# S5 parameter set-up beside the projections, modulation rows in four column tiles, and three smaller edits in a hybrid diffusion step

## The reference

```python
mod = silu(cond) @ ada_w[l] + ada_b[l]                  # two conditions: c_ctx and c
proj = h @ ev_w_in                                      # layer 0: 2048 columns
# S5: 32 groups of 16 channels, 64 complex states, two directions
lam_bar = exp(lam * exp(log_step)); b_bar = ((lam_bar - 1) / lam) * B
bu = b_bar @ u;  hs = scan(lam_bar, bu);  y = Re(C @ hs) + d * u
y = gelu(y);  y = y * sigmoid(y @ glu_w + glu_b)
# mLSTM, per head, direction and chunk of 128 tokens
dmat = where(causal, b[t] - b[s] + i[s], -inf)
s = (q @ k.T) * exp(dmat - mq);  num = s @ v + w_inter * (q @ cm)
cm_new = keep * cm + (w_s * k).T @ v                    # the final states are outputs too
```

## Time and profile before

| | us |
|---|---|
| median of 3 runs | 5072.52 (5072.29 to 5074.31) |
| the profiled execution | 5074.22 |
| its span | 5072.4 |
| PE busy | 4520.9 (89%) |
| DVE busy | 2916.7 (58%) |
| POOL busy | 1705.2 (34%) |
| ACT busy | 799.7 (16%) |

### The profile page before, as it was taken

One profiled execution on the slowest core, in us unless ns is written; L12 is line 12 of the kernel. 1 busy time (PEld: TensorE's weight loads), 2 busy tenths in 40 slices (PEclk: granted clock), 3 DMA queues, 4 the chain that ended last, 5 costly groups with the idle time before them and its releaser, 6 DMA issues. The chain is left out here.

```text
span 5072.4 us, 43983 instructions
## 1 busy us (share of the span) xinstructions
PE 4520.9 (89%) x15098; PEld 2543.0 (50%) x15098; DVE 2916.7 (58%) x5806; ACT 799.7 (16%) x1626; POOL 1705.2 (34%) x1616
## 2 busy tenths in 40 slices
PE   6798766897799999999997998688879999999997
PEld 2453233475645545555444677456655555555453
DVE  4424752298636756665684405449853765666477
ACT  1211232103700000000002213110550000000000
POOL 0000541003805645555550000000551565555464
PEclk8899988899999999999998998799999999999998
DMA  3120423112638989999891110221454998999896
GB/s 135 46 81 31 146 86 123 66 55 89 178 133 322 368 312 394 353 365 351 335 370 59 66 42 0 54 75 46 133 170 160 351 367 331 378 366 351 305 404 270
DMA packets 354240, 1048.43 MB, mean 207 GB/s; under 512 B 31689, under 2 KB 132505, under 8 KB 342330
## 3 DMA queue, kind: packets, MB, share of 16 engines
q0 software_dynamic: 148128, 545.35, 28.4%
q1 hardware_dynamic: 106844, 450.27, 24.0%
q10 hardware_dynamic: 99072, 50.33, 3.5%
HBM read 991.70 MB, written 54.14 MB: 206 GB/s over the span
## 5 line engine op out<-in xcount | busy, mean ns | idle before, releaser
L598 PE MATMUL banks<-blocks,dense_weight 128*128 128x512 f32 x3072 | 1377.4, 599 | 51.3 <-DVE dense_weight L773 51.3
L565 PE MATMUL banks<-h_dense_T,blocks 128*128 128x384 f32 x4096 | 1363.6, 487 | 37.7 <-DVEq L666 37.7
L565 PEld LDWEIGHTS banks<-h_dense_T,blocks 128*128 128x128 f32 x4096 | 779.8, 191 | 628.8 <-issue 111.3
L598 PEld LDWEIGHTS banks<-blocks,dense_weight 128*128 128x128 f32 x3072 | 589.3, 192 | 755.3 <-issue 697.0
L409 POOL DMA_INDIRECT expert_rows<-in_pk_u_dram,expert x512 | 649.4, 1268 | 797.4 <-DVE own_dots L788 352.1
L409 POOL DMA_INDIRECT expert_rows<-in_pk_v_dram,expert x512 | 601.1, 1174 | 491.2 <-DVE acc L807 203.0
L773 DVE TENSOR_TENSOR dense_weight<-dense_act,shared 128x384 f32<-128x384 f32 x256 | 218.4, 854 | 802.4 <-PE banks L598 738.1
L807 DVE SCALAR_TENSOR_TENSOR acc<-expert_rows,expert_weight,acc 128x1024 f32<-128x1024 f32 x504 | 624.4, 1284 | 64.6 <-DMA expert_rows<-in_pk_v_dram,expert 64.1
L788 DVE CUSTOM_DVE_ANT_0 expert_rows<-expert_rows,h_rows 128x1024 f32<-128x1024 f32 x512 | 595.0, 1221 | 0.1
L444 ACT ACTIVATE dense_act<-banks 128x384 f32<-128x384 f32 x256 | 125.5, 490 | 2356.5 <-PE banks L565 2346.7
L400 POOL TENSOR_SCALAR shared<-iota,picked_T 128x128 f32<-128x128 f32 x192 | 120.6, 642 | 522.2 <-ACT picked_T L450 460.3
(11 more groups left out here) (461 smaller groups left out, 4660.9 us busy)
## 6 DMA issues: line engine op xcount, KB each, us to landing
blocks<-in_pk_u_turned_dram SPq DMA_DIRECT2D x256, 512.0 KB, 6.3
blocks<-in_pk_v_dram SPq DMA_DIRECT2D x256, 512.0 KB, 6.8
gates_dram<-shared ACTq DMA_DIRECT2D x48, 1024.0 KB, 5.1
shared<-gates_dram SPq DMA_DIRECT2D x32, 1536.0 KB, 10.8
ada_block<-in_ada_rest_dram SPq DMA_DIRECT2D x32, 1280.0 KB
blocks<-in_pk_w_q_dram SPq DMA_DIRECT2D x32, 512.0 KB, 3.6
w_block<-in_ev_w_in_dram SPq DMA_DIRECT2D x16, 512.0 KB, 3.5
expert_rows<-in_pk_u_dram,expert POOLq DMA_INDIRECT x512, 7.8
```

Source lines behind the costliest of these rows:

```text
L565: mm = pe.matmul(dense_dots(c), u[:, k * P:(k + 1) * P], HT[:, k, :], start=(k == 0), stop=(k == KD - 1))
L598: mm = pe.matmul(ps[:, at_:at_ + HALF], wt[:, c % WEIGHED, z * P:(z + 1) * P], v[:, half_ * HALF:(half_ + 1) * HALF], start=(c == 0), stop ...
```

## The change

- The S5 parameter set-up moves out of s5 into even_inputs. A new function s5_parameters runs on DVE behind the last short convolution; its sines stand on ACT between the two last pairs of drains; its parameter DMAs are issued by SP behind the first two weight blocks and the taps. What is kept lies in a new class S5Parameters, the scratch in MIXT.
- readouts moves from POOL to DVE. DVE's function scans is cut in two: turn_in (rotate in) and scans. For a quad m of 1 or more the order on DVE is turn_in(m), readouts(m), inputs(m+1), scans(m). Eight of the 16 copies of US into its rearranged form move from ACT to DVE. POOL is left with clearing, angles and decays.
- The modulation rows become 16 blocks of 640 columns, each loaded in two halves of four eighths of the width. Each eighth is four products of 160 columns, written to PSUM partitions 0, 32, 64 and 96 (four column tiles of PE), and ACT takes four copies per row. Each quad has four rows, and none stand ahead or at the end.
- inside(m) writes the products of its four pairs to the same four column tiles of one bank; ACT copies s_M straight from PSUM in 16 copies, and the buffer s_K is gone.
- The token columns of even_inputs, s5_gate and mlstm_inputs are cut into 320 + 320.
- In mlstm_cells one product of 256 columns masks both heads, and a second one adds minus the maximum of both heads, from negM2, which two DVE operations make for each pair. That leaves four products per direction.
- The store of the final mLSTM states waits for the first step of the last pair (state_set) rather than for the end of the last step's rest.

```diff
-MOD_W = 320
+MOD_W = 640
...
+            for dst, src in ((s.par, "s5_par"), (s.B, "s5_B"), (s.C, "s5_C"), (s.d32, "s5_d")):
+                sp.dma_start(dst[:], T[src]).then_inc(par_in, 16)
...
-                    pe.matmul(ps[:, at:at + LAT], lhs, HT[:, k, CTX:TOK],
-                              start=(k == 0), stop=(k == KD - 1))
-                    mm = pe.matmul(ps[:, at + HALF:at + HALF + CTX], lhs, HT[:, k, 0:CTX],
-                                   start=(k == 0), stop=(k == KD - 1))
+                    for c in range(2):
+                        mm = pe.matmul(ps[:, at + c * HALF:at + c * HALF + EVEN], lhs,
+                                       HT[:, k, c * EVEN:(c + 1) * EVEN],
+                                       start=(k == 0), stop=(k == KD - 1))
...
+            act.wait_ge(phi_set, 1)
+            act.activation(phi[7][:], phi[0][:], ACT.Sin, scale=6.283185).then_inc(sines_done, 1)
+            act.activation(phi[8][:], phi[0][:], ACT.Abs).then_inc(sines_done, 1)
+            act.wait_ge(sines_done, 2)
+            act.activation(phi[8][:], phi[8][:], ACT.Sin, bias=s.quarter[:], scale=-6.283185
+                           ).then_inc(sines_done, 1)
...
+            s5_parameters(line, dve, s, phi, par_in, phi_set, sines_done)
...
+def s5_parameters(line, dve, s, phi, par_in, phi_set, sines_done):
...
+    exact_exp(dve, one, dt[:], par[:, 2, :], w1[:], w2[:], whole[:])
...
+    exact_exp(dve, one, r[:], lr[:], fr[:], fi[:], whole[:])
...
-                b, at = n % 2, MOD_FIRST + n * MOD_W
+
+                w = T["ada_rest"][n // 2].rearrange("p (h x) -> p h x", h=2)
                 if n >= 2:
                     sp.wait_ge(ada_used, n - 1)
-                sp.dma_start(ada[:, b, :], T["ada_rest"][n]).then_inc(ada_in[b], 16)
-                sp.dma_start(ada_b[:, b, :], T["ada_b"][:, at:at + MOD_W]).then_inc(ada_in[b], 16)
+                sp.dma_start(ada[:, n % 2, :], w[:, n % 2, :]).then_inc(ada_in[n % 2], 16)
+                if n % 2 == 0:
+                    at = MOD_FIRST + n // 2 * MOD_W
+                    sp.dma_start(ada_b[:, n // 2 % 2, :], T["ada_b"][:, at:at + MOD_W]
+                                 ).then_inc(ada_in[0], 16)
...
+            for m in range(QUADS):
+                angles(m)
                 line.settle()
-                pool.sem_inc(c_set, 1)
-
-            pool.wait_ge(phi_set, 1)
-            angles(0)
-            pool.wait_ge(pow_set, 1)
-            line.settle()
-            decays(0)
-            angles(1)
-            for m in range(QUADS):
-                pool.wait_ge(angle_set, min(m + 2, QUADS))
-                readouts(m)
-                if m + 1 < QUADS:
-                    decays(m + 1)
-                if m + 2 < QUADS:
-                    angles(m + 2)
+                decays(m)
...
             def inside(m):
-                for h in range(2):
-                    act.wait_ge(k_raw, 2 * m + h + 1)
-                    act.activation(K[:, 2 * h:2 * h + 2, :],
-                                   ps[0:2 * S5C, (K0, K1)[h]:(K0, K1)[h] + 448].rearrange(
-                                       "p (i c) -> p i c", i=2), ACT.Copy).then_inc(k_copied, 1)
-                act.wait_ge(k_copied, 2 * m + 2)
-                for j in range(T4):
-                    act.activation(M[32 * j:32 * j + 32, :, :],
-                                   K[:, :, 32 * (3 - j):32 * (3 - j) + P], ACT.Copy
-                                   ).then_inc(m_set, 1)
+                act.wait_ge(k_raw, m + 1)
+                for i in range(4):
+                    for j in range(T4):
+                        at = K0 + 32 * (3 - j)
+                        act.activation(M[32 * j:32 * j + 32, i, :], ps[32 * i:32 * i + 32, at:at + P],
+                                       ACT.Copy).then_inc(m_set, 1)
...
             def ada_row(n):
-                b = n % 2
-                pe.wait_ge(ada_in[b], 32 * (n // 2 + 1))
-                if n:
-                    pe.wait_ge(ada_copied, n)
-                for k in range(KD):
-                    pe.matmul(ps[0:2, ADA0:ADA0 + MOD_W], cond_s[:, k, :],
-                              ada[:, b, k * MOD_W:(k + 1) * MOD_W], start=(k == 0), stop=False)
-                pe.matmul(ps[0:2, ADA0:ADA0 + MOD_W], ones[:], ada_b[:, b, :],
-                          start=False, stop=True).then_inc(ada_used, 1)
+
+                for h in range(2):
+                    pe.wait_ge(ada_in[h], (32 - 16 * h) * (n + 1))
+                    if h == 0 and n:
+                        pe.wait_ge(ada_copied, 4 * n)
+                    for k in range(KD // 2):
+                        for j in range(4):
+                            at = k * MOD_W + ADA_COLS * j
+                            mm = pe.matmul(ps[32 * j:32 * j + 2, ADA0:ADA0 + ADA_COLS],
+                                           cond_s[:, KD // 2 * h + k, :], ada[:, h, at:at + ADA_COLS],
+                                           start=(h == 0 and k == 0), stop=False)
+                    if h == 0:
+                        mm.then_inc(ada_used, 1)
+                for j in range(4):
+                    mm = pe.matmul(ps[32 * j:32 * j + 2, ADA0:ADA0 + ADA_COLS], ones[:],
+                                   ada_b[:, n % 2, ADA_COLS * j:ADA_COLS * (j + 1)],
+                                   start=False, stop=True)
+                mm.then_inc(ada_used, 1)
...
-                for i in range(4):
-                    at = (K0, K1)[i // 2] + (i % 2) * 224
-                    for d in range(2):
-                        for part in range(2):
-                            pe.matmul(ps[0:2 * S5C, at:at + 224],
+                for d in range(2):
+                    for part in range(2):
+                        for i in range(4):
+                            pe.matmul(ps[32 * i:32 * i + 32, K0:K0 + 224],
                                       BL[:, m % 2, part, 4 * d + i, 3 - 3 * d, :],
                                       CL[:, part, 4 * d + i, d:d + 7, :].rearrange("p s j -> p (s j)"),
                                       start=(d == 0 and part == 0), stop=False)
-                    mm = pe.matmul(ps[0:2 * S5C, at + 96:at + 128], ident[0:2 * S5C, 0:2 * S5C],
-                                   diag[:, 4 * m + i, :], start=False, stop=True)
-                    if i % 2 == 1:
-                        mm.then_inc(k_raw, 1)
+                for i in range(4):
+                    mm = pe.matmul(ps[32 * i:32 * i + 32, K0 + 96:K0 + 128],
+                                   ident[0:2 * S5C, 0:2 * S5C], diag[:, 4 * m + i, :],
+                                   start=False, stop=True)
+                mm.then_inc(k_raw, 1)
...
-            n = ada_rows(0, ADA_EARLY)
+            n = 0
             for m in range(QUADS):
                 turn(m)
                 n = ada_rows(n, 1)
...
                 n = ada_rows(n, 1)
                 if m:
                     outputs(m - 1)
+                n = ada_rows(n, 1)
                 inside(m)
-                n = ada_rows(n, 3)
-            n = ada_rows(n, ADA_LATE)
...
+            def readouts(m):
...
+                        if m:
+                            dve.wait_ge(y_raw, 4 * m)
...
+                            line.count(tt(CL[h, part, k, slots, cols_of(gr)],
+                                                          first[h, k], second[h, k], ALU.subtract))
+                line.settle()
+                dve.sem_inc(c_set, 1)
...
             inputs(0)
+            for j in range(T4):
+                for i in range(2, 4):
+                    dve.tensor_copy(UP[32 * j:32 * j + 32, :, i, :],
+                                    US[32 * i:32 * i + 32, :, j::T4]).then_inc(u_by_dve, 1)
+            dve.tensor_tensor(diag[:], ident[0:2 * S5C, 0:2 * S5C].unsqueeze(1).to_broadcast(
+                [2 * S5C, PAIRS, 2 * S5C]),
+                s.d32[:, :].unsqueeze(2).to_broadcast([2 * S5C, PAIRS, 2 * S5C]), ALU.mult
+                ).then_inc(diag_set, 1)
+            dve.wait_ge(diag_set, 1)
+            inputs(1)
             for m in range(QUADS):
-                if m + 1 < QUADS:
-                    inputs(m + 1)
+                if m == 0:
+                    readouts(0)
+                turn_in(m)
+                if m:
+                    readouts(m)
+                    if m + 1 < QUADS:
+                        inputs(m + 1)
                 scans(m)
...
-            sp.wait_ge(tail_done, pairs * NT + 1)
+            sp.wait_ge(state_set, (pairs - 1) * (NT + 1) + 2)
...
+                    pe.matmul(es[:, d, :, 0, :], ident[:],
+                              mask[:, d, :].unsqueeze(1).to_broadcast([P, 2, P]),
+                              start=True, stop=False)
+                    pe.matmul(es[:, d, :, 0, :], ones8[:], negM2[:, :, d, tile],
+                              start=False, stop=True)
                     for h in range(2):
-                        pe.matmul(es[:, d, h, 0, :], ident[:], mask[:, d, :],
```

(8 more changed lines are left out.)

381 lines of the change are left out of this document (193 added, 188 removed).

## The result

The changed kernel takes 4903.21 us, median of 4 runs (4899.71 to 4904.48), against 5073.42 before (again four runs): ratio 0.9661, interval 0.9645 to 0.9678. The profiled execution has 4903.42 us, its span 4901.7, so 170.7 us of span are gone.

| stretch | before | after | gained |
|---|---|---|---|
| start to the first S5 clearing | 491.1 | 487.4 | 3.7 |
| S5 | 373.6 | 233.9 | 139.7 |
| S5 to the mLSTM recurrences | 2160.5 | 2155.9 | 4.6 |
| mlstm_cells, first copy of columns to the last step's end | 188.3 | 176.4 | 11.9 |
| from there to the next stage's first DVE operation | 19.7 | 1.1 | 18.5 |

A forecast was written before the change was run, and what follows sets the result against it. S5 was held bound by a chain of waits with no engine full, and by DVE after the change. Gains of 147 (S5), 18 (state store) and 9 (scores), together 174, took 5074.2 to 4900 us; range 4862 to 4980.

The forecast's parts named there:

- DVE becomes the bound of S5: S5: DVE, at 44.2 us per full quad against PE's 40, sets the stage's end at 718; 147 us gained.
- first rotation: DVE's first rotation in S5, behind angles, tables, turn and into_states: comes at about 528, 44 us earlier than before.
- four quads: DVE's quads in S5: 158.9 us of work together, plus 4 us per quad for waits.
- The row: A modulation row on PE in S5: 36 products, half the serial time saved by tiles, about 5.5 us with tile change.
- second rival: S5: all four column tiles run together, DVE never waits, S5 ends at 702; range 4862 to 4885 us; chance .10.
- first rival: S5: column tiles do nothing, PE bounds at 62.8 us per quad; 4951 us, range 4930 to 4970; chance .28.
- The read-outs: Read-out matrices on DVE in S5: 6.9 us per quad; PE's wait before inside gone or below 5 us.
- The set-up, hidden: S5 parameter set-up on DVE beside the projections: 27 us, hidden in DVE's idle time; at worst 6 us lost.
- the early rows: Eight modulation rows filling PE before S5's first turn; removing the set-up there gains only if they go too.
- The smaller edits: State store 18 us gained, mLSTM scores net 9, token columns of 320 + 320 zero.
- fourth rival: S5: PE, working serially with pauses, stays at 1.2 GHz; quad 108 us, whole time 5132 us; chance .03.
- ring: S5's 71.4 us period per quad: outputs, POOL's read-outs, inside, three rows, turn, into_states, DVE's rotations and scans, outputs.

The follow-up runs named there:

- e1: Changed kernel with the products of each modulation row half and of inside ordered one column tile after the other; 4908.45 us.
- e12: Changed kernel with modulation rows on two alternating column tiles of 320 columns instead of four of 160; 4908.42 us.
- e6: Changed kernel without POOL's angles of the second to fourth quad, leaving out part of the computation; 4878.16 us.
- e8: Changed kernel with modulation rows serial, as two groups of 320 columns, each through the whole width before the other; 4990.62 us.
- e2: Changed kernel with the read-out matrices formed by POOL again, in its order of before; 4910.74 us.
- e9: Changed kernel with serial rows of two 320-column groups and the read-out matrices on POOL again; 4987.46 us.
- e3: Changed kernel with the parameter set-up back at the head of DVE's work in S5, its loads still early; 4928.04 us.
- e7: Changed kernel with all copies of US on ACT and the first three quads' angles on POOL during the Hyena stage; 4878.90 us.

## Why the prediction was right, step by step

**DVE becomes the bound of S5: right.** The trace shows it, and e1 and e12 show it by doubling PE's rows at the cost of 6 and 2.4 us of S5. The stage gained 139.7 us where 147 were forecast. That the sum comes so close is in part luck: the first rotation came 18 us late and the four quads took 11.5 less, and neither was foreseen.

**The first rotation: 18 us late.** Counted from the first clearing (491.08 before, 487.35 after) it was to come at 37 and came at 55.2. The path that the prediction added up, from POOL's angles through the tables, the turn and into_states to the copies, held within 5 us: MIXT was complete at 528.66, 41.3 behind the clearing. What came later was DVE itself, whose own queue up to there was not added up: the first input matrices took 13.8 where 5.5 was the price of a quad's, the eight copies 14.26 where nothing was put down for them, s_diag and the second input matrices 12.9, the read-outs 6.9. Much of it is POOL's doing: e6 has the rotation at 44.0 without the later angles.

**The four quads: 11.5 us faster.** From the first rotation to the end of DVE's work it took 163.5 us, where 175 were forecast: 158.9 of work and 16 of waits. The work came out at 158.6, the waits at 4.9, of which 4.23 stand before the last rotation. So it is the allowance for waits and for POOL, 4 us per quad, that was too large; the loss beside POOL fell ahead of the first rotation, where nothing was allowed. The work agrees by luck. The prediction's scans of 22.5 us were read from a quad in which POOL was at work; they take 28.1 beside POOL's angles (551.97 to 580.1), in the first two quads, and 16.6 and 15.6 in the last two, which makes 88.5 for four times 22.5. That POOL would be done in two quads was right.

**The row: 2.7 us, not 5.5.** The reason given, that only neighbours of two products could overlap, is wrong: two tiles give 10.0 / 5.1 = 2.0, four give 10.0 / 2.7 = 3.7. The second rival, all four tiles at once and DVE never waiting, was nearly right in both; its end of S5 at 702 misses the 18 us of the first rotation and the 5 of waits, and with these added it comes to 725, where S5 did end if it is counted from the clearing of before (491.1 and 233.9). The Trainium skill's three column tiles at 2.38 ("TensorE: Matmul & The Clock Gate", section "Measured speedup vs the span model") lie somewhat below what these runs give per tile.

**The first rival was priced too low.** With rows of 10 us S5 lasts 318 us, not 278, and the time is 4990, outside that rival's 4930 to 4970: PE's pauses ahead of rows were not in its sum. Some 9 us per quad of them are waits for loads, which come from the way in which e8 takes its loads, so e8 is not that rival alone.

**The read-outs: 6.9 us on DVE, right** (535.49 to 542.3). PE's wait before inside came down from 18.18 to 6.54, a little above the 5 that were said. That their place would matter as much as the wait of 18.18 suggested was not shown: e2 and e9 put its worth at 10 and 2 us of S5, e9 with the reservation above. One row more now stands between outputs and inside, where PE had waited; every run keeps a row there, so what this order alone is worth stays open.

**The set-up, hidden: right.** It ran from 322.4 to 351.4 us, 29 where 27 were said, and the Hyena convolution began at 358.19, 2 us earlier than before. Its removal from S5 is worth 26 us by e3. The prediction tied that gain to the early rows, which are gone in e3 too, so no run shows that tie.

**The smaller edits.** The store gained 18.5 (18 said), the scores 11.9 (9 said): a step's scores take 3.40 us for 4.22, .82 less where .7 was assumed, an estimated 16.4 over 20 steps, so that some 4.5 would be the price of the two DVE operations per pair. PE's wait at the start of a pair has grown by something of that size, from 4.83 us (at 3122.51 before) to 6.52 (at 2924.37), over four pairs. The token columns gained nothing, as said.

**PE's clock.** The granted clock in S5 is .75, against .86 before; PE is now busy for 128 of 235 us, where it was for 260 of 375. As DVE bounds the stage, that should cost little, and e12 agrees: there PE is busy for 159 us of the same window at a clock of .83, and S5 is no shorter. The fourth rival needed PE as the bound.

## What to carry to other kernels

A wait in the trace names the last link of a ring, not the one to shorten: here the wait was for POOL's read-outs, and moving them is worth 10 us by e2, the short rows in the same ring up to 84 by e8. When an engine is to become the bound, add up its own queue from its first operation on, and read its durations from a stretch in which its neighbours do what they will do after the change. Two products that need the same copy to be done should not become neighbours.

## What was not expected of the hardware

Column tiles overlap nearly in full when neighbouring products lie on different tiles (a row of 10.0 us takes 5.1 on two and 2.7 on four), and still by a factor of 1.8 (10.0 to 5.5) in blocks of four products on one tile. DVE beside POOL loses more than the pair of rotations that the prediction read (11.74 and 5.97 us): two operations on s_Bl, each with two inputs in SBUF, went from 1.41 to 5.01 us beside POOL's tensor operations, and took 1.40 again when POOL stood still (at 533.94). While POOL was only clearing (until 495.4), DVE's operation of .69 kept its length. The Trainium skill says as much in "SBUF — State Buffer", section "Who interferes with whom": DVE operations with two SBUF inputs collide with POOL's reads, not with its writes. What is left open is how the loss would divide if POOL's operations were shorter: e7's half-sized ones were not compared alone.
